# Two of GpSimd's weight sums start behind a VectorE matrix

## The reference, cut to what matters

```python
(dn_q, dn_k, dn_v, dn_b, dn_a, dn_z, sw_q, sw_k, sw_v, xa_q, gates) = jnp.split(h @ w_in, split_idx, axis=-1)
o_dn = deltanet_branch(dn_q, dn_k, dn_v, dn_b, dn_a, dn_z, dn_conv_w, dn_a_log, dn_dt_bias, dn_norm_w)
...
gates = jax.nn.sigmoid(gates.reshape(B_, S_, N_BRANCH, D))
merged = jnp.sum(gates * jnp.einsum('bsnc,ncd->bsnd', branches, w_branch), axis=2)
```

```python
a = jnp.where(strict, jnp.einsum('bhncd,bhnsd->bhncs', k_beta, k) * decay, 0.0)
t_mat = a + jnp.eye(C, dtype=f32)
sol = lax.linalg.triangular_solve(t_mat, rhs, left_side=True, lower=True, unit_diagonal=True)
```

## Time and profile before

| | us |
|---|---|
| median of 3 runs | 3063.53 |
| fastest and slowest of them | 3063.14 and 3064.57 |
| the profiled execution, whole | 3068.0 |
| its span, first to last instruction | 3066.2 |
| TensorE busy in the span | 2886.4 |
| VectorE busy in the span | 2016.5 |
| GpSimd busy in the span | 783.6 |

### The profile page before, as it was taken

How to read it: one execution, slowest core, us unless ns; L and a number is a source line. 1 busy time by engine, 2 the same in 40 slices (tenths; PEclk the granted TensorE clock), 3 DMA queues, 4 the chain that set the end, 5 groups by cost and what they waited for, 6 DMA issues and landing times.

```text
span 3066.2 us, 38895 instructions
## 1 busy us (share of the span) xinstructions
PE 2886.4 (94%) x14660; PEld 1936.6 (63%) x14660; DVE 2016.5 (66%) x4447; ACT 996.4 (32%) x2628; POOL 783.6 (26%) x672
## 2 busy tenths in 40 slices
PE   9999999999999999999999988888989998888877
PEld 9957897995985889798685533333448553333322
DVE  7753664776774657477576867666656686666665
ACT  1113231110101224021164444444445454444443
POOL 0010340000001044000013544444421354444442
PEclk9999999999999999999999999999999999999999
DMA  6443333554454323455458999999995799999998
GB/s 245 170 172 137 118 111 124 180 185 160 176 180 158 131 99 118 143 200 212 153 212 328 421 421 421 421 421 421 421 388 203 290 421 421 422 421 421 422 421 360
DMA packets 120283, 831.69 MB, mean 271 GB/s; under 512 B 13472, under 2 KB 16032, under 8 KB 21792
## 3 DMA queue, kind: packets, MB, share of 16 engines
q0 software_dynamic: 74592, 536.90, 42.2%
q1 hardware_dynamic: 43920, 282.74, 26.0%
q10 hardware_dynamic: 1584, 9.56, 0.8%
HBM read 828.10 MB, written 1.05 MB: 270 GB/s over the span
## 4 chain that ended last, share of the span: by engine, by line
PE 66%; DMA 20%; DVE 6%; ACT 6%; issue 1%; POOL 0%; ACTq 0%; POOLq 0%; SPq 0%; DVEq 0%
DMA arena<-table_uv,idx 15%; PE bank L2880 13%; PE bank L540 12%; PE bank L630 8%; PE bank L439 6%; DMA ring<-table_uv,idx 5%; PE bank L527 4%; PE bank L801 4%; PE bank L1065 3%; PE bank L2556 2%; ACT diag L3158 2%; PE bank L2748 2%; PE bank L466 2%; DVE arena L3589 1%; PE bank L2591 1%
## 5 line engine op out<-in xcount | busy, mean ns | idle before, releaser
L2880 PE MATMUL bank<-arena,diag 128*128 128x512 f32 x1316 | 641.5, 613 | 99.7 <-ACT diag L3158 92.6
L3589 DVE CUSTOM_DVE_ANT_0 arena<-arena 128x1024 f32<-128x1024 f32 x330 | 403.4, 1225 | 233.8 <-DMA arena<-table_uv,idx 233.5
L2880 PEld LDWEIGHTS bank<-arena,diag 128*128 128x128 f32 x1316 | 230.1, 190 | 420.4 <-ACT diag L3158 243.5
L3703 POOL DMA_INDIRECT arena<-table_uv,idx x324 | 356.3, 1100 | 487.0 <-PE bank L2880 400.4
L2880 PE MATMUL bank<-ring,diag 128*128 128x512 f32 x728 | 357.9, 618 | 59.9 <-ACT diag L3158 57.7
L3138 ACT ACTIVATE dots<-dots 128x1 f32<-128x1 f32 x512 | 103.5, 202 | 639.6 <-DVE dots L3589 638.7
L3589 DVE CUSTOM_DVE_ANT_0 ring<-ring,arena 128x1024 f32<-128x1024 f32 x182 | 222.7, 1224 | 131.6 <-DMA ring<-table_uv,idx 131.3
L2880 PEld LDWEIGHTS bank<-ring,diag 128*128 128x128 f32 x728 | 128.9, 192 | 238.8 <-ACT diag L3158 141.0
L2086 POOL TENSOR_TENSOR x_tok<-arena,ktail 128x1024 f32<-128x1024 f32 (+1 forms) x10 | 22.0, 2198 | 1001.7 <-ACT arena L1094 1001.7
L3703 POOL DMA_INDIRECT ring<-table_uv,idx x182 | 206.7, 1136 | 237.4 <-PE bank L2880 224.6
L3158 ACT ACTIVATE diag<-cst,dots 128x128 f32<-128x128 f32 x504 | 202.4, 402 | 47.8 <-PE bank L2880 1.1
(11 more groups left out here) (765 smaller groups left out, 5027.1 us busy)
## 6 DMA issues: line engine op xcount, KB each, us to landing
ring<-stream SPq DMA_DIRECT2D x237, 1024.0 KB, 4.9
ktail<-ln_rows ACTq DMA_DIRECT2D x6, 1024.0 KB, 5.2
arena<-stream SPq DMA_DIRECT2D x6, 1024.0 KB, 9.7
arena<-table_uv,idx POOLq DMA_INDIRECT x336, 21.1
ring<-table_uv,idx POOLq DMA_INDIRECT x182, 20.8
arena<-mem_rows SPq DMA_DIRECT2D x2, 1024.0 KB, 9.7
more<-stream SPq DMA_DIRECT2D x2, 1024.0 KB, 8.6
cst<-stream SPq DMA_DIRECT2D x2, 1024.0 KB, 8.3
```

What stands on the lines that cost most here:

```text
L2880: last = mm(bank[4 + 2 * tt + half][:, :], diag[:, n % DIAGS, :], row_slot(l, n)[:, D + 512 * half:D + 512 * half + 512], start=(h == 0 an ...
L3589: v.tensor_tensor_reduce(u, u, tok[:, tt, :], 1.0, 0.0, ALU.mult, ALU.add, dots[:, tt, k:k + 1]).then_inc(u_used.sem, 1)
L3703: g.indirect_dma_start(out=row_slot(l, n), out_offset=None, in_=peer_uv, in_offset=number).then_inc(row_loaded[PLACE[l][n]], 16)
```

## The change

In each of the two layers of the first block, GpSimd's sets 0 and 1 also wait until VectorE's first masked chunk matrix of that layer is written.

```diff
                 pool.wait_ge(loaded.sem, loaded.at(l, 16 * (slab // RING + 1)))
                 if j == 0:
                     pool.wait_ge(silu_done.sem, silu_done.at(l, 12))
+                if j in (0, 1):
+                    pool.wait_ge(lt_ready.sem, lt_ready.at(l, 1))
                 if j == GATE_OWN + 1:
                     pool.wait_ge(uw_done.sem, uw_done.at(l, 4))
```

## The result

The change made the kernel slower: 3070.93 us median of nine runs (3069.52 to 3074.45) against 3064.06 us of nine runs of before (3063.14 to 3064.57). The ratio is 1.0024 with an interval of 1.0015 to 1.0033, +6.9 us by the medians. The profiled execution of the changed kernel has a span of 3067.7 us and a whole time of 3069.52, the fastest of its runs.

A forecast was written before the change was run, and what follows sets the result against it. TensorE was taken as the bound, busy 1053.49 of 1060.00 us. Two layers of stall and clock less layer 1's loss, 2 x (3.0 + 1.3) - 5.77 = +2.8, on the median 3063.53 gave 3066.4 us, range 3060.6 to 3071.0.

The forecast's parts named there:

- The step that failed: Layer 1, ahead of line 833: a 2.81 us TensorE wait and 2.96 us of lower clock go, 5.77 us gained.
- the prediction's own sum: Both layers' new stall and lower clock less layer 1's present loss: 2 x (3.0 + 1.3) - 5.77 = +2.8 us.
- the wrong set: Layer 1, VectorE's `qdec` and `lt`: set 0 running over them was said to cost 3.0 us.
- Rival C: Layer 1's late slab landing occurs only in the profiled execution, so the change only costs: +8.6 us, 3072; chance 0.2.
- B: Both new stalls of 3.3 us are followed by 2.96 us of lower clock: +6.8 us, 3070.3; chance 0.07.
- D: Timed runs collide in both layers, so 2 x 5.77 goes: -2.9 us, 3060.6; chance 0.1.
- The stall: Ahead of `gate_half(0)`, both layers: TensorE waits for the delayed set 0, 3.0 us each, bounds 1.9 to 3.3.
- `Y` goes first and set 0 is held twice: Behind `lt`: shared port lock lets `Y`, then `level_part(1)`, hold set 0, 0.69 us each, making it 6.4 us.
- The clock: Behind each new wait at `gate_half(0)`: TensorE at half clock, 1.7 us at three chances in four, 1.3 per wait.
- `gate_half(2)` never waited for set 1: At `gate_half(2)`: set 1 runs some 6.5 us later, cover shrinks from 8.8 to about 5 us, no wait.

The follow-up runs named there:

- set 0 late in layer 0: Kernel before the change, with GpSimd doing the first subtraction of set 0 twice in layer 0; 3067.38 us, ratio 1.0009.
- the filled stall: The changed kernel with 5 unused TensorE products ahead of `gate_half(0)`; 3069.79 us, ratio 1.0016 against the kernel before the change.
- before again: Kernel before the change, run again without any edit; 3064.63 us, ratio 0.9998.
- runs with 12: The changed kernel with 12 unused TensorE products ahead of `gate_half(0)`; 3074.03 us, ratio 1.0031 against the kernel before the change.
- `qdec` later: Kernel before the change, with VectorE's two `qdec` products moved behind `level_part(1)`, no new wait; 3065.60 us, ratio 1.0003.

## Why the prediction was wrong

It said no measurable change (+2.8 us, 3066.4, at a chance of 0.77), and the kernel became 6.9 us slower, 3070.93, at the very end of the range.

**The step that failed** is the gain: "Gain: 5.77 us, in layer 1 alone". The mechanism was right in kind: the wait and the lower clock did go. The size was taken from one execution that happened to show it large. In three other profiled executions in which layer 1 stands as before, it lost 1.68 (above), 1.77 and 1.75 us. TensorE in layer 1 of the run with the waits in layer 0 only, and of the run with set 0 late in layer 0:

```profile
1088.77 3.72 PE L734 MATMUL bank<-x,ring 128*128 128x256 f32 x16
1094.19 1.15 PE L833 MATMUL bank<-cst,lt 64*64 64x64 f32 x32 [1.70 <-DVE lt L1827]
...
1108.56 1.95 PE L801 MATMUL bank<-gate_x_sums,hid 128*128 128x128 f32 x16
```

```profile
1088.42 3.72 PE L734 MATMUL bank<-x,ring 128*128 128x256 f32 x16
1093.82 1.15 PE L833 MATMUL bank<-cst,lt 64*64 64x64 f32 x32 [1.68 <-DVE lt L1827]
...
1108.19 1.95 PE L801 MATMUL bank<-gate_x_sums,hid 128*128 128x128 f32 x16
```

With 1.7 in place of 5.77, the prediction's own sum, 2 x (3.0 + 1.3) - 1.7, gives +6.9. That it meets the measured +6.9 to the tenth is luck: the interval reaches from +4.6 to +10.1, and the filled stall leaves another clock term (below). A warning was there and was weighed too low: the profiled execution of before took 3068.0 us, 4.5 above the median of the runs, and 5.77 - 1.7 is 4.1.

The gain was also put down to the wrong set in part. The prediction saw set 0 behind all 3.0 us that VectorE lost. Set 0 was over at 1086.80, before the second `qdec` product began at 1087.27; that product and `lt` met set 1. With set 1 alone held back, layer 1's loss is 0.48. So where layer 1 loses 1.7, holding set 0 as well, at a stall of 2.98 per layer, has some 0.5 left to gain.

**Rival C** had the right end (the change mostly costs), at a chance of 0.2, with the wrong cause. It blamed the late landing of set 0's slab. That landing is late in layer 1 when before runs again as well, 6.1 us from issue to landing against 5.1 in layer 0, and layer 1 still lost 1.7. What came and went is the start of set 1, which its slab's landing sets, 0.2 us earlier or later.

**Rivals B and D.** B's number, +6.8, lies nearest to the measured one, but its mechanism did not come: it needs 5.77 to gain and 2.96 us of lower clock behind each new stall, and no profile shows more than 1.63 there. D, collisions in both layers, is not borne out: layer 0 lost nothing in the profiled executions of before, of before again and of the run with the waits in layer 1 only.

**The stall**: 3.0 was forecast from set 1's row, 2.74 of wait measured, 2.98 as a loss. Set 0 took 5.75 us, not the 6.1 behind the 3.0, and nearly 0.3 passed between `lt`'s end and its start and between its end and TensorE's, which the forecast left out; the two errors nearly cancel. `Y` took its undisturbed 0.69, and set 0's first instruction 1.69 instead of 1.27; `level_part(1)` took 0.79, and set 0's third instruction 0.3 more than alone. The prediction had worked out from the Trainium skill, SBUF — State Buffer, section Who interferes with whom, that `Y` goes first and set 0 is held twice, for 0.69 us each. The trace agrees on the order and on two holds, but they cost 0.42 and 0.31, less than that estimate.

**The clock**: 1.3 per stall was forecast. The profiles show 1.63 (layer 0 of the change, and of the run with the waits there) or nothing (layer 1 of both kernels with a stall there). The change at +6.9 and the filled stall at +4.9 leave 1.0 per stall. Their intervals overlap, so this size is not settled by the runs; that the clock falls after some of these stalls only is shown by the profiles. The spread of the times points the same way: the change's runs have a standard deviation of 1.7 us and those with the waits in layer 0 only 1.4, the filled stalls 0.6 and 0.7, and before 0.6 to 0.9. Why the clock fell in layer 0 and not in layer 1 is open.

**The rest.** `gate_half(2)` never waited for set 1 in the change, and layer 0, undisturbed before, lost most (4.61 of the profiled losses). One other stretch did give time back in the change's profiled execution: from `gate_half(2)` of layer 0 to `project(12)` of layer 1 it took 723.94 us, against 725.26 in that of before and 725.02 to 725.19 in the other eight. So this belongs to the one execution and not to the waits, and is part of why it was the fastest of its nine.

Left open: how often the large loss occurs in timed runs. The runs with 12 and with 5 products and with `qdec` later exclude it as the typical case. None of the nine runs of before in the first session reached 3065, and none of those of the other sessions the 3068.0 of that profiled execution, which speaks for its being rare, but no timed run shows its rows.

## What to carry to other kernels

A saving that is read from one execution has to be checked against the runs' median first: when the profiled execution is slower than the median by about the size of the saving, the saving may be what made it slower. A wait that keeps a helper engine out of the way should hold only the work whose result is wanted late: in layer 0 set 1 had almost 9 us to spare, set 0 had 5 and was held for 7. When two layers run the same text and only one shows a stall, look for the start that differs by tenths of a us.

## What the hardware showed unexpectedly

The meeting of GpSimd and VectorE goes in steps: 0.2 us in the start of one GpSimd instruction (2.84, 2.88 against 3.01, 3.07 and 3.09 after zero) decided, in five meetings, whether the two `qdec` products took 3.25 and 3.18 us or 2.13, 2.05 and 2.15. In the first two cases the GpSimd instruction began 0.21 and 0.10 us ahead of the second product and was through before it; in the other three it began 0.01 to 0.15 us behind it and was the one held. The second thing is the clock: waits of 2.74 and 2.75 us at the same place, behind the same work, were followed by half clock (0.50) in one layer and by full clock (1.00) in the other.
